# Slot order of the split weights, a bias table moved between two units, and sums of squares moved from GpSimd to VectorE

## The reference

```python
x = x + 0.5 * swiglu(rms(x), w_ffn1_gu, w_ffn1_down)             # FFN 1
x = x + mixer1(rms(x) @ w_in) @ w_out                            # gated recurrence + local attention
x = x + 0.5 * swiglu(rms(x), w_ffn2_gu, w_ffn2_down)             # FFN 2
x = x + rms(even_mixer(rms(x)))       # mixer 2: 3-tap convolution + dilated attention with a bias by distance
x = x + rms(conv_ffn(rms(x)))         # FFN 3: g = 3-tap convolution of h @ w_g; (silu(g) * u) @ w_down
x = x + rms(odd_mixer(rms(x)))        # mixer 3: 31-tap convolution, layer norm + stick-breaking attention
x = x + rms(conv_ffn(rms(x)))         # FFN 4
```

## Time and profile before

| what | value |
|---|---|
| median of 3 runs | 2534.14 us (2532.8 to 2534.89) |
| the profiled execution's own time | 2534.05 us |
| its span in the trace | 2532.1 us |
| TensorE, matmuls | busy 2374.5 us, 94% of the span, 10780 of them |
| VectorE | 1345.5 us, 53% |
| ScalarE | 992.2 us, 39% |
| GpSimd | 364.4 us, 14% |
| chain that ended last | 80% TensorE, 9% VectorE, 4% issue, 3% ScalarE, 2% SyncE's queue |

### The profile page before, as it was taken

How to read it: one execution, slowest core, us unless ns; L and a number is a source line. 1 busy time by engine, 2 the same in 40 slices (tenths; PEclk the granted TensorE clock), 3 DMA queues, 4 the chain that set the end, 5 groups by cost and what they waited for, 6 DMA issues and landing times.

```text
span 2532.1 us, 31274 instructions
## 1 busy us (share of the span) xinstructions
PE 2374.5 (94%) x10780; PEld 1902.5 (75%) x10780; DVE 1345.5 (53%) x1828; ACT 992.2 (39%) x1478; POOL 364.4 (14%) x281
## 2 busy tenths in 40 slices
PE   8999999999998799999989989999987967999998
PEld 6888887677776688888867677887875746788787
DVE  5444335565655544443445475554269985655423
ACT  4222225656666432232234443333233434433322
POOL 0111002334443011110000011110011220211100
PEclk9999999999999899999999999999998978999999
DMA  4233322222222123233222122223211112122231
GB/s 163 93 99 108 102 73 87 102 80 80 70 70 95 50 92 99 94 112 101 69 84 92 59 83 92 99 92 113 86 68 58 59 34 67 67 99 91 100 107 51
DMA packets 61604, 217.77 MB, mean 86 GB/s; under 512 B 7600, under 2 KB 12208, under 8 KB 61536
## 3 DMA queue, kind: packets, MB, share of 16 engines
q1 hardware_dynamic: 60368, 214.76, 25.5%
q10 hardware_dynamic: 1168, 2.12, 0.3%
HBM read 214.73 MB, written 2.12 MB: 86 GB/s over the span
## 4 chain that ended last, share of the span: by engine, by line
PE 80%; DVE 9%; issue 4%; ACT 3%; SPq 2%; DMA 1%; POOL 1%; DVEq 0%; ACTq 0%; POOLq 0%
PE bank L1666 25%; PE bank L1668 25%; PE bank L1667 25%; DVE m_acc L1258 3%; SPq L190 2%; DMA raw<-in_w_in 1%; DVE wL L1659 1%; PE bank L551 1%; DVE m_later L1245 1%; PE bank L541 1%; PE bank L527 1%; ACT m_prob L240 0%; PE bank L598 0%; PE bank L973 0%; PE bank L983 0%
## 5 line engine op out<-in xcount | busy, mean ns | idle before, releaser
L1666 PE MATMUL bank<-H,wH 128*128 128x512 f32 x3012 | 1207.8, 401 | 66.3 <-DVE wL L1659 28.1
L1667 PE MATMUL bank<-L,wH 128*128 128x512 f32 x3012 | 1187.3, 394 | 0.0
L1668 PE MATMUL bank<-H,wL 128*128 128x512 f32 x3012 | 1186.4, 394 | 0.0
L1659 DVE TENSOR_TENSOR wL<-raw,wH 128x1024 fp32r<-128x1024 f32 (+1 forms) x357 | 489.1, 1377 | 667.4 <-ACT wH L1654 667.4
L1666 PEld LDWEIGHTS bank<-H,wH 128*128 128x128 f32 x3012 | 575.0, 191 | 202.5 <-issue 50.4
L1667 PEld LDWEIGHTS bank<-L,wH 128*128 128x128 f32 x3012 | 575.7, 191 | 121.1 <-issue 4.3
L1668 PEld LDWEIGHTS bank<-H,wL 128*128 128x128 f32 x3012 | 574.1, 191 | 122.8
L1654 ACT ACTIVATE wH<-raw 128x1024 fp32r<-128x1024 f32 (+1 forms) x357 | 391.4, 1105 | 273.0 <-PE bank L1668 221.5
L1959 POOL TENSOR_TENSOR silu_g<-silu_g,rstd 128x512 f32<-128x512 f32 x88 | 113.8, 1294 | 886.8 <-ACT silu_g L1848 473.2
L1859 ACT ACTIVATE H<-prod 128x512 f32 (+1 forms) x88 | 55.7, 632 | 262.7 <-DVE prod L1912 262.7
L1892 DVE TENSOR_TENSOR gate_s<-bank,rstd 128x512 f32<-128x512 f32 x88 | 60.7, 690 | 99.0 <-PE bank L1668 95.9
(11 more groups left out here) (255 smaller groups left out, 1752.7 us busy)
## 6 DMA issues: line engine op xcount, KB each, us to landing
raw<-in_w_ffn_gu SPq DMA_DIRECT2D x88, 512.0 KB, 3.4
raw<-in_w_in SPq DMA_DIRECT2D x56, 512.0 KB, 4.2
raw<-in_w_ffn_down SPq DMA_DIRECT2D x32, 704.0 KB, 4.2
raw<-in_w_up_2a SPq DMA_DIRECT2D x44, 512.0 KB, 3.4
raw<-in_w_up_2b SPq DMA_DIRECT2D x44, 512.0 KB, 3.4
raw<-in_w_in_even SPq DMA_DIRECT2D x24, 512.0 KB, 4.7
raw<-in_w_down_2a SPq DMA_DIRECT2D x16, 704.0 KB, 4.2
raw<-in_w_down_2b SPq DMA_DIRECT2D x16, 704.0 KB, 4.1
```

The source lines that it names most:

```text
L1659: dve.tensor_tensor(w_l, raw_at(st, j), w_h.bitcast(F32), ALU.subtract).then_inc(S.lo_done, 1)
L1666: pe.matmul(out, w_h, xh[:, k0 + k], start=start and k == ks[0], stop=False)
L1667: pe.matmul(out, w_h, xl[:, k0 + k], start=False, stop=False)
L1668: last = pe.matmul(out, w_l, xh[:, k0 + k], start=False, stop=stop and k == ks[-1])
```

## The change

1. GU3 and GU4 use the slots (2, 3) first and then (0, 1, 2, 3); OUT2 and OUT3 ahead of them get (2, 3, 0, 1). 
2. At the start of FFN 3 and 4 the splits of units (1,2) and (1,3) each move ahead in the order of ScalarE and VectorE.
3. The table of mixer 2 is made between units (0,3) and (0,4) by `pe_table`; `dve_scaled` 3 and 4 move ahead of `split_lo` of unit (1,0).
4. Unit (1,0) of the three mixers waits for each tile of the normal activation by itself, and in mixer 3 its splits move ahead of `normal_act` and `normal_dve`.
5. The 7 adds of squares at each post-norm entry are made by VectorE in `enter_dve`; `enter_pool` is gone.

```diff
@@ Stream
         if extra is not None:
-            self.first = (0, 1, None, None, 2)[:per]
-            self.split = {4: (2, 3, 0, 1), 5: (3, 0, 1, 2, 1)}[per]
+            self.first = {4: (2, 3, None, None), 5: (0, 1, None, None, 2)}[per]
+            self.split = {4: (0, 1, 2, 3), 5: (3, 0, 1, 2, 1)}[per]
@@ build
-    OUT2 = Stream(t["w_out_even_2"], 2, 4, 8, early=True)
+    OUT2 = Stream(t["w_out_even_2"], 2, 4, 8, early=True, split=(2, 3, 0, 1))
...
-    OUT3 = Stream(t["w_out_odd_2"], 2, 4, 8, early=True)
+    OUT3 = Stream(t["w_out_odd_2"], 2, 4, 8, early=True, split=(2, 3, 0, 1))
@@ all three mixers, pe
+    def v_ready(pe):
+        return lambda f: pe.wait_ge(S.v_ready, site.v0 + f + 1)
...
-                if isinstance(u, int) and u == 1 and j == 0:
-                    pe.wait_ge(S.v_ready, site.v0 + DT)
...
-                    k.unit_product(pe, st, u, j, bank[st.bank[j]][:], k.HL, site.v, True, True)
+                    k.unit_product(pe, st, u, j, bank[st.bank[j]][:], k.HL, site.v, True, True,
+                                   v_ready(pe) if isinstance(u, int) and u == 1 and j == 0 else None)
@@ mixer 2, dve
+            if isinstance(p, int) and p == 0:
+                dve_scaled(dve, 3)
+                dve_scaled(dve, 4)
             slot(0)
             if isinstance(p, int) and p == 0:
-                for j in (3, 4, 5):
-                    dve_scaled(dve, j)
+                dve_scaled(dve, 5)
@@ mixer 2, pe
+    def pe_table(pe):
+
+        pe.wait_ge(M.tab_in, 48)
+        pe.wait_ge(M.evac, 3)
...
+            if isinstance(u, int) and u == 0:
+                pe_table(pe)
             unit(4)
...
         body(-1, True, False, False)
-        pe.wait_ge(M.tab_in, 48)
-        pe.wait_ge(M.evac, 3)
...
         pe.wait_ge(M.tab_sum, 2)
         body(0, True, True, False)
@@ mixer 3, act and dve
         evac(act, 0, 1)
+        k.split_hi(act, st, 1, 0)
         k.normal_act(act, site, 0, DT)
...
         for j in range(PER - 1):
             dve_scaled(dve, j)
+        k.split_lo(dve, st, 1, 0)
         k.normal_dve(dve, site, 0, DT)
@@ enter_dve
+            def add_square2(n):
+                dve.wait_ge(S.sq2_done, b + n + 1)
+                if n > 1:
+                    dve.wait_ge(S.ssq2_done, 7 * c.posts + n - 1)
+                dve.tensor_tensor(ssq[:], square[:, 0] if n == 1 else ssq[:], square[:, n % 2], ALU.add)\
+                   .then_inc(S.ssq2_done, 1)
...
                 if n >= 1:
                     scaled_lo(dve, site, n - 1)
+                if n >= 2:
+                    add_square2(n - 1)
@@ ffn_act, start of FFN 3 and 4
+            if site.lead == 4:
+                split_hi(act, st, 1, 2)
+                gate(0, 1)
+                up(0, 1)
+                split_hi(act, st, 1, 3)
+                gate(1, 0)
+                up(1, 0)
+            else:
+                body(1, 0)
@@ ffn_dve, start of FFN 3 and 4
+            if site.lead == 4:
+                gate(0, 1)
+                low(0, 0)
+                split_lo(dve, st, 1, 2)
+                taps(0, 1)
+                product(0, 1)
+                split_lo(dve, st, 1, 3)
+                gate(1, 0)
+                low(0, 1)
+                taps(1, 0)
+                product(1, 0)
+            else:
+                body(1, 0)
```

More of the change, by code:

```diff
@@ L984, in pe_probT @@
         last.then_inc(M.p_tr, 1)
+    def pe_table(pe):
+        pe.wait_ge(M.tab_in, 48)
+        pe.wait_ge(M.evac, 3)
+        pe.matmul(bank[6][0:8, 0:HALF_W], buckets[0:32, 0:8], buckets[0:32, 8:8 + HALF_W], start=True, stop=True)\
+          .then_inc(M.tab_mm, 1)
+        pe.matmul(bank[7][0:8, 0:DIST - HALF_W], buckets[0:32, 0:8], buckets[0:32, 8 + HALF_W:8 + DIST], start=True,
+                  stop=True).then_inc(M.tab_mm, 1)
     def pe_pv_pair(pe, p, i):
@@ L1162, in slot @@
             def slot(j):
-                if units and not (isinstance(u, int) and u == 0 and j < st.early):
+                if units and not (isinstance(u, int) and (u == 0 and j < st.early or u == 1 and j == 0)):
                     k.split_hi(act, st, u, j)
@@ L1436, in unit @@
                     return
-                if isinstance(u, int) and u == 1 and j == 0:
-                    pe.wait_ge(S.v_ready, site.v0 + DT)
-                else:
+                if not (isinstance(u, int) and u == 1 and j == 0):
                     back = next(b for b in range(1, PER + 1) if st.bank[(j - b) % PER] == st.bank[j])
@@ L1783, in enter_dve @@
                 split_lo(dve, st, i, j)
[L1785 to L1793, removed]
         def normal_act(act, site, lo, hi):
@@ L1864, in body @@
             def body(i, ip):
[L1865 to L1869, removed]
+                split_hi(act, st, i, 0)
+                gate(ip, 1)
+                split_hi(act, st, i, 1)
+                up(ip, 1)
+                split_hi(act, st, i, 2)
+                gate(i, 0)
+                split_hi(act, st, i, 3)
+                up(i, 0)
+            if site.lead == 4:
[7 more added lines that the diff above has]
+                body(1, 0)
             with act.Fori(2, st.bodies) as i:
@@ L1917, in low @@
                                   ALU.subtract).then_inc(S.a_ready, 1)
-            def split(i, j):
-                if not (isinstance(i, int) and site.lead == 4 and j < 2):
-                    split_lo(dve, st, i, j)
             gate(0, 0)
@@ L1927, in body @@
             def body(i, ip):
-                split(i, 0)
+                split_lo(dve, st, i, 0)
                 gate(ip, 1)
@@ L1931, in body @@
                 taps(ip, 1)
-                split(i, 1)
+                split_lo(dve, st, i, 1)
                 product(ip, 1)
-                split(i, 2)
+                split_lo(dve, st, i, 2)
                 gate(i, 0)
@@ L1937, in body @@
                 taps(i, 0)
-                split(i, 3)
+                split_lo(dve, st, i, 3)
                 product(i, 0)
-            body(1, 0)
+            if site.lead == 4:
[11 more added lines that the diff above has]
+                body(1, 0)
             with dve.Fori(2, st.bodies) as i:
@@ L2371, in _ @@
                     mixers[rest[1]].pool(pool)
-                elif rest[3].st is not None and rest[3].post is not None:
-                    enter_pool(pool, c, rest[3])
 INPUTS = ("xT", "cols", "ident", "heads1", "win_mask", "gate_w", "rpb", "rel_bias_2", "dist_onehot", "dist_add", "before",
```

## The result

The changed kernel takes **2509.69 us**, median of 4 runs (2506.29 to 2510.63), against 2533.74 us for the kernel before in the same comparison (4 runs, 2532.80 to 2534.89). The ratio is 0.9902, with a 95% interval of 0.9885 to 0.992: 24.05 us less. The profiled execution took 2510.1 us, its span is 2508.3 us and its granted clock 0.972 of full speed (2532.1 and 0.965 before).

The account below looks back on a forecast made before the run. The prediction took TensorE, busy for 94% of the span, to bound the kernel, with VectorE setting mixer 3's pace. Its terms summed to 23.0 us less, giving 2511 us, with a range of 2504 to 2520.

Parts of the forecast that it names:

- Bound of the kernel: Whole kernel: a change is worth TensorE's idle and slow time removed, nothing where another engine sets the pace.
- Ends of FFN 3 and 4: First splits of DN3 and DN4 start before the last product ends: gain 5.0 us in FFN 3, 4.8 in FFN 4.
- Table of mixer 2: Ahead of body 1 of mixer 2: the earlier table removes the 7.18 us wait and slow clock; gain 9.9 us.
- The new wait on `M.evac`: In `pe_table`, mixer 2: its condition is met at 1264.3, while TensorE comes at 1267.1.
- OUT2: Last body of mixer 2: split of OUT2 (0,1) no longer delays the probabilities' copy; gain 1.0 us, from below 0.
- Start of FFN 3 and 4: The 2.35 us wait at unit (1,2) becomes 1.6 at (2,0), with a clock drop of 1.7; gain 0.9 each.
- Adds: Post-norm entries: squares added on VectorE end TensorE's small hold-ups; gain 0.5 us in all, from 0 to 1.0.
- Rival 3: Post-norm entries: the adds cost VectorE their own length and it sets the pace; 12.8 us less gain, 2524; 4%.
- Mixer 3: VectorE sets its pace, so the 9.75 us wait moves ahead of unit (1,1); gain 0.
- rival 1: Mixer 3 gives its 9.75 us of idle time back too, with the slow clock; 2499 us; 7%.
- Sum: Whole kernel: 5.0 + 4.8 + 9.9 + 1.0 + 1.8 + 0.5 = 23.0 us gained, so 2511 us.
- Rival 2: Clock still drops at FFN ends and mixer 2; FFN starts and OUT2 give nothing: 13.8 us gained, 2520; 13%.

Follow-up runs that it names:

- e5: Changed kernel with unit (1,0) of mixer 3 as before: split behind the normal tiles, one wait for all eight; 2510.12 us.
- e8: Changed kernel with 28 in place of 31 convolution taps in mixer 3, so its output is another; 2500.81 us.
- e1: Changed kernel with the old slot orders of GU3, GU4, OUT2 and OUT3; 2519.72 us.
- e11: Same edit as e1 on the changed kernel, run once more for its profile; 2518.84 us in one run.
- e2: Changed kernel with the table's matmuls (`pe_table`) of mixer 2 put back behind body 0; 2517.92 us.
- e9: Changed kernel with four in place of two `probT` buffers in mixer 2; 2510.13 us.
- e6: Changed kernel with the old order at the start of FFN 3 and 4, split of unit (1,2) behind the second gate; 2514.88 us.
- e4: Changed kernel with the 21 adds of squares on GpSimd again; 2510.64 us.
- e10: Changed kernel with the edits of e7 and e9 together; 2504.62 us.
- e7: Changed kernel with the split of unit (1,3) moved further ahead at the start of FFN 3 and 4; 2504.79 us.
- e3: Changed kernel with `dve_scaled` 3 and 4 back behind `split_lo` of unit (1,0), the table still early; 2512.84 us.

## Why the prediction was right

**Bound of the kernel.** Right: each gain is idle or slow time of TensorE that went, and the stage with VectorE as its pace gave nothing (e5, e8).

**Ends of FFN 3 and 4.** The mechanism is shown by e1: the slots make the first split wait. Between the two traces it gave 5.05 and 5.03, against 5.0 and 4.8. What the terms claimed is only partly the edit's, though: 3.45 follow from it wherever it was tried; the slow matmuls, 1.5 to 1.7, were in the kernel before and in neither profile of its order undone (e1, e11).

**Table of mixer 2.** 9.82 against 9.9; e2 gives 7.7 for its place alone. With the lead of 0.9 added back, the sum comes at 1271.1 (1271.1 predicted) and the low split ends at 1276.9 (1277). The new wait on `M.evac` did not show.

**OUT2: the step that failed.** "Gain 1.0" took the split ahead of the copy for the whole cause. Behind it stood a second one: the copy waits for the product that still reads its `probT` buffer, and 0.14 was won. e9 took that away too, and 0.47 was left, the exposed copy of a single bank.

**Start of FFN 3 and 4: mis-sized.** 0.9 each was predicted; e6 measures 1.33 and 1.43. The 1.7 for a clock drop behind the smaller wait was wrong, since none came, and the 0.9 us at (2,1) was left out: in the kernel before, TensorE arrived there 4 us later and the lateness was covered. The two errors have opposite signs.

**Adds.** 0.36 at the entry of mixer 3 and 0.1 in FFN 3, against 0.5 in all. The hold-ups were as small as predicted, but the term is not shown as a gain of the kernel: mixer 3 gives part back, and undone alone (e4) nothing is left by the end. Rival 3 is refuted by e4.

**Mixer 3.** 0 predicted, -0.11 measured; rival 1 is refuted by e5.

**Sum.** 22.99 from the changed stretches, 23.0 predicted. The errors of -0.9 (OUT2), about +0.8 (starts and entries), +0.3 (ends), -0.1 (table) and -0.1 (mixer 3) cancel; that the sum fits so well is luck. So is part of the 5.0 at each FFN end, of which undoing the order took back only some 3.45 (e1, e11). Rival 2 described OUT2 rightly and the rest wrongly.

**What stays open:** why the clock fell behind 3.17 us of idle time in the kernel before, and not behind the same 3.17 in e1 and e11. Both windows of e1 lie at a DMA load like that of the earlier trace rows (0.55 against 0.61, 0.54 against 0.53), so the DMA load alone does not explain it. e9 and e10 show the same difference in the same code, so it may be no property of the kernel at all. How often the clock falls differs by place: behind the 2.55 us at the end of mixer 2 in 12 of 13 profiles, behind the 2.35 at the FFN starts in 4 of 4 (the kernel before, e6), behind the 3.17 at the FFN ends in 2 of 6. What sets this the runs do not show.

## What to carry to other kernels

Read a wait as a list, not as one releaser: when the cause named is removed, the next condition on the same instruction decides, so look in the trace when each of them was met (OUT2: 0.14 of 0.97). A wait that moves to a later unit can be shortened again by the same means, by putting the split where its engine stands idle anyway (e7, another 4.9 us). Count idle time as sure and the slow matmuls behind it as likely at best (12 of 13 at one place, 2 of 6 at another), and undo a part in the changed kernel before believing its share of the gain.

## What the runs showed of the hardware

- Of idle stretches of TensorE: behind 1.41 us at unit (2,0) the clock stayed at 1.00, in FFN 3 and 4 of all nine profiles that have this wait; behind 2.34 it was 0.55 (e6), behind 5.95 it was 0.54 (e2); behind 2.55 it was 0.52 in e9 and 1.00 in e10, in the same code, and low in 12 of 13 profiles; behind 3.17 it was 0.51 and 0.59 in one kernel and 1.00 at four places of e1 and e11. The length of the stretch alone does not decide.
- Mixer 1, whose code is the same in the changed kernel and all eleven runs, differs from profile to profile: at the first matmul behind it (near 862 us) the eleven were from 0.5 to 4.3 us later than the changed one, the kernel before 0.9. In part it shows as a lower mean clock and fewer matmuls in the same 360 us. Windows 500 to 860 of TensorE, the changed kernel and then e9:

```profile
500.00:860.00 360.00, 322.88 (x1553) 0.95 0.23 76
```

```profile
500.00:860.00 360.00, 325.84 (x1544) 0.93 0.23 77
```

  In others the delay lies elsewhere: e4, 3.4 us later, has 0.95 and 1554 matmuls in this window. So medians that differ by 2 to 3 us (e3) or 5 (e6) say little of where the time went, and the leads stage by stage say more.
- A GpSimd add of 1.85 us makes VectorE operations of 0.75 us take 1.78 (e4), and over an entry VectorE is better off with the adds itself: 20.70 us for 31 operations in place of 22.85 for 24.
